# Column groups for two small projections, a closer order of the new states, and another order of the first expert loads

## The chip, the cores and the metric

The kernel runs on one core of a Trainium2 chip. The metric is the device time of one execution in microseconds (us). Before the change it is 1283.96 us, the median of three runs (1283.41 to 1284.04).

## What is computed

One layer of a hybrid decoder for 288 tokens: 256 of a prompt (two tiles of 128 rows, tile 0 and tile 1) and 32 of eight samples (tile 2). All of it is fp32. The parts that matter here:

```python
z, xbc, dt_raw, q, k, v = split_in(rmsnorm(h) @ w_in)        # dt_raw: 16 of 4112 columns
dt = softplus(dt_raw + dt_bias)                               # one step size per token and head
y_ssd, new_ssm = ssd_chunked(x, dt, -exp(a_log), B, C, old_state)
...
h = h + concat(y_ssd, attention) @ w_out
logits = rmsnorm(h) @ router_w + router_b                     # 32 columns, one per expert
top_val, top_idx = top_k(logits, 4)
...
h = h + sum over the chosen experts of gate * (swiglu(x @ w1[e] + b1[e]) @ w2[e] + b2[e])
```

There are 32 experts; w1 of one is 1024x2048 and w2 is 1024x1024, together 12.6 MB, so the experts' weights are 403 MB of the 476 MB that the kernel moves.

## The kernel before

Each engine has one program, and they meet at counting semaphores; the order on each engine is written out by hand. Time runs through four stages.

1. *Projections and attention* (to about 232 us). The list STEPS (made by mixer_steps) is walked by TensorE, VectorE and ScalarE alike. A step "proj" is eight matmuls of 288 columns, "kscore" sixteen matmuls of 288 columns whose outputs lie in four groups of 32 partitions (L1735), "pv" four matmuls of 512 columns, again in four groups of 32 (L1767), "pv_new" and "gather_o" end a group of samples, "p_score", "p_trans" and "p_out" are the prompt's attention by head. The step "dt" (L1786) takes, for each of the three tiles, eight matmuls: the stationary operand is a 128x128 block of the normed tokens xnT (128x32 for tile 2), the moving one is 16 columns of w_dt. VectorE then turns the sums into dt and dA by a chain of small operations (L1210 to L1229) with two looks at ScalarE (L887, L889), and GpSimd starts on x*dt when dt_ready is there (L652 to L655). PSUM bank 2 is shared with the steps "nat" and "conv_out".
2. *Scan and states* (to about 270 us).
3. *Output projection, new states and router* (to 351 us). mixed(c, half, order, between) is twelve matmuls of 512 columns (L1988) for one tile and one half of the columns; the dictionary between names what TensorE does ahead of its i-th matmul. In tile 0's calls these are new_states(0) to new_states(7), which make the samples' eight new states by rounds (TensorE L1911, VectorE L1317, where a round must be taken out of banks 4 and 5 before the next is written), mix_turn (transposes of the mixed rows, L1966, taken out by mixT_evac), and last_state. In tile 1's calls they are the router: router(c, ks), eight matmuls with a 128x128 block of tokens stationary and 32 columns of w_router moving (L2004), and prefix(c, s). VectorE's choose(c, s) waits for the logits, picks the four experts and signals mask_ready; prefix sums the masks; first_places gives each token its place and signals S_ready; gather_tile (L2022) then gathers the tokens of the first two experts. The last tile to be routed is tile 1.
4. *Experts* (from 351 us). Eight turns of four experts. SyncE loads units of 2 MB (six per expert, four of w1 and two of w2) into eight places; unit 8 and each one after it waits until TensorE has used the unit that lies in its place (expert_slot_used). Units 5, 6 and 7 wait for the last matmuls of mixed(1, 1). Units 0 to 3 need the places of the states, of z and of the attention's buffers: the order is 3, store_states(0), store_states(1), 0, 2, 1, 4, 5, ... by the loop below. Units 0 and 1 go where the samples' states lay, four samples each, so these have to be stored first.

```python
for n in [3, 0, 2, 1] + list(range(4, PER_EXPERT * TURN)):
    if n == 0:
        store_states(0)
        sp.wait_ge(sem("ssm_s_out"), 16 * 4)
        store_states(1)
    ...
    unit_load(e, e, j)
```

Of the kernel before, what the change touches and what calls it, by code (L numbers as in the profile page):

```python
# [11 lines left out]
ALU = mybir.AluOpType  # L12
# [124 lines left out]
def mixer_steps():  # L137
# [58 lines left out]
    steps.extend(("pv", t) for t in range(4, 8))  # L196
    steps.extend([("pv_new", 0), ("p_trans", 0), ("p_score", 1)])
# [52 lines left out]
def hymba_step(nc, a, o):  # L250

    ctx = ExitStack()
    with ctx:
# [65 lines left out]
        w_dt = d3(take(KT * H), H)  # L319
        w_router = d3(take(KT * NE), NE)  # L320
        vecs = take(36)
# [50 lines left out]
        edx = r_small[:, 144:160]  # L372
        row_max = d3(r_small[:, 0:16], DB)
# [146 lines left out]
        def _(sp):  # L520
# [222 lines left out]
        def _(act):  # L743
# [98 lines left out]
            for kind, i in STEPS:  # L842
# [41 lines left out]
                elif kind == "dt":  # L884

                    act.wait_ge(sem("dt_dve"), 1)
                    nc.scalar.activation(dts[:, 144:192], dts[:, 96:144], ACT.Exp, scale=-1.0).then_inc(sem("dt_act"), 1)  # L887
                    act.wait_ge(sem("dt_dve"), 2)
# [148 lines left out]
        def _(dve):  # L1037
# [73 lines left out]
            for kind, i in STEPS:  # L1111
# [92 lines left out]
                elif kind == "dt":  # L1204

# [3 lines left out]
                    dve.wait_ge(sem("dt_ps"), 1)  # L1209
                    nc.vector.tensor_copy(d3(vecs[:, 28:36], W1_ROWS), ps[:, 2, 48:56].rearrange("p (o s) -> p s o", o=W1_ROWS))  # L1210
                    link(nc.vector.tensor_tensor(d3(raw[:, 0:32], H), d3(ps[:, 2, 0:32], H), bvec[:, 0:16].unsqueeze(1).broadcast_to([P, 2, H]), ALU.add))
                    link(nc.vector.tensor_tensor(raw[0:NS, 32:48], ps[0:NS, 2, 32:48], bvec[0:NS, 0:16], ALU.add))
                    link(nc.vector.tensor_scalar(u1, raw, -1.0, None, ALU.mult))
                    nc.vector.tensor_tensor(u1, u1, raw, ALU.max).then_inc(sem("dt_dve"), 1)
                    dve.wait_ge(sem("dt_act"), 1)
                    nc.vector.tensor_scalar(u1, e1, 1.0, None, ALU.add).then_inc(sem("dt_dve"), 1)
                    dve.wait_ge(sem("dt_dve"), 2)
# [5 lines left out]
                    dve.wait_ge(sem("dt_act"), 2)  # L1223
# [207 lines left out]
            def choose(c, s):  # L1431

                n = ROWS[c]
                dve.wait_ge(sem("rstd_ready"), s + 2)
                dve.wait_ge(sem("logit_ps"), s + 1)
                link(nc.vector.scalar_tensor_tensor(logit[0:n, c, :], ps[0:n, LOGIT_BANK[c], 0:NE], stat[0:n, 20 + c:21 + c], bvec[0:n, 48:80], ALU.mult, ALU.add))
# [57 lines left out]
            row_scale(0, 0)  # L1494
# [3 lines left out]
            row_scale(2, 1)  # L1498
# [10 lines left out]
            row_scale(1, 2)  # L1509
# [100 lines left out]
        def _(pe):  # L1610
# [59 lines left out]
            def turn_waits():  # L1670
# [5 lines left out]
                elif turn[0] == "dt":  # L1676
                    pe.wait_ge(sem("dt_dve"), 1)

            for kind, i in STEPS:
# [99 lines left out]
                elif kind == "dt":  # L1779
# [3 lines left out]
                    nc.tensor.transpose(ps[:, 2, 48:56], rows_small[32:40, 0:P], ident[32:40, 32:40])  # L1783
# [266 lines left out]
            mixed(0, 1, natural, {1: lambda: new_states(3), 2: before_1, 4: lambda: new_states(4), 5: lambda: mix_turn(1, 1), 6: lambda: new_states(5),  # L2050
# [218 lines left out]
```

## Time and profile before

| | us |
|---|---|
| median of three runs | 1283.96 |
| the profiled execution's own time | 1286.54 |
| its span, first to last instruction | 1284.5 |
| TensorE busy (share of the span) | 1239.8 (97%) |
| VectorE, ScalarE, GpSimd busy | 383.6, 232.1, 49.2 |
| DMA moved, mean rate | 476.2 MB, 371 GB/s |

The profiled execution is 2.6 us longer than the median of the runs, and 2.0 us of it lie outside the span. A busy share is a mean over stages with different limits. "PEclk" is TensorE's granted clock, 1.00 being 2.4 GHz and 0.50 being 1.2 GHz. A matmul in fp32 stands in the rows as two instructions, so x16 are eight matmuls; transposes are one each. Rows of the timeline overlap at their ends, as matmuls are pipelined: what a group costs is best read from its start to the start of the next.

### The profile page before, as it was taken

What the parts mean: (1) busy time and instruction counts of PE and PEld (TensorE: products, weight loads), DVE (VectorE), ACT (ScalarE), POOL (GpSimd) and SP (SyncE); (2) the same over time, 40 slices, a digit from 0 to 9 for tenths busy, and PEclk for the clock granted to TensorE, in tenths of its full rate; (3) what the DMA queues carried; (4) which work ended last, traced back from release to release, by engine and by line L of the source; (5) the groups of instructions that cost most, each with busy time, mean ns of one, the idle gap of its engine ahead of it and who ended that gap; (6) DMA issues with size and microseconds to landing.
All of it is one profiled execution on the core that took longest, in us unless ns stands there. A gap on an engine that the chain in (4) does not pass through costs nothing.

```text
span 1284.5 us, 14702 instructions
## 1 busy us (share of the span) xinstructions
PE 1239.8 (97%) x5752; PEld 524.4 (41%) x5752; DVE 383.6 (30%) x768; ACT 232.1 (18%) x473; POOL 49.2 (4%) x46
## 2 busy tenths in 40 slices
PE   9999999999999999999999999999999999999997
PEld 6766665544433333333333333333333333333332
DVE  2478522674421222212132121212122221212122
ACT  2013333544201111110111011010111110110102
POOL 0000030513000000000000000000000000000000
PEclk8999989999999999999999999999999999999999
DMA  9697768336899999999999999999999999999992
GB/s 278 210 323 265 248 232 316 149 123 255 371 381 427 430 427 430 426 430 427 431 427 431 426 432 426 432 426 431 427 429 428 429 429 428 429 428 428 428 428 114
DMA packets 67294, 476.20 MB, mean 371 GB/s; under 512 B 7688, under 2 KB 25380, under 8 KB 40412
## 3 DMA queue, kind: packets, MB, share of 16 engines
q1 hardware_dynamic: 65134, 471.87, 89.5%
q10 hardware_dynamic: 1582, 2.03, 0.5%
q0 software_dynamic: 544, 1.84, 0.4%
q8 instruction: 23, 0.38, 0.1%
q14 instruction: 11, 0.09, 0.0%
HBM read 468.47 MB, written 7.24 MB: 370 GB/s over the span
## 4 chain that ended last, share of the span: by engine, by line
PE 72%; DMA 24%; DVE 2%; ACT 1%; issue 1%; SPq 0%; DVEq 0%
DMA ring<-in_w 23%; PE ps L2180 22%; PE ps L2222 13%; PE ps L1692 9%; PE ps L2128 7%; PE ps L1988 3%; PE ps L1735 1%; PE ps L2136 1%; PE ps L2112 1%; PE ps L2120 1%; PE ps L2198 1%; PE ps L2171 1%; PE ps L1767 1%; PE ps L1911 1%; PE ps L1711 1%
## 5 line engine op out<-in xcount | busy, mean ns | idle before, releaser
L2180 PE MATMUL ps<-ring,own 128*64 128x512 f32 x1536 | 340.9, 593 | 17.2 <-DMA ring<-in_w 17.2
L1581 DVE TENSOR_SCALAR own<-ps 128x512 f32<-128x512 f32 x32 | 22.2, 692 | 650.0 <-PE ps L2180 650.0
L2180 PEld LDWEIGHTS ps<-ring,own 128*64 128x64 f32 x1536 | 108.6, 137 | 236.6 <-issue 197.2
L2222 PE MATMUL ps<-ring,own 128*64 128x512 f32 x768 | 172.7, 599 | 3.5 <-ACT own L1018 3.4
L1692 PE MATMUL ps<-own,ring 128*128 128x288 f32 x512 | 132.5, 413 | 1.3 <-DVE own L1074 1.1
L2180 PE MATMUL ps<-own 128*64 128x512 f32 x512 | 115.8, 593 | 2.4 <-DMA own<-in_w 2.4
L1692 PEld LDWEIGHTS ps<-own,ring 128*128 128x128 f32 x512 | 96.2, 192 | 32.2 <-issue 4.5
L1014 ACT ACTIVATE own<-own 128x512 f32<-128x512 f32 x32 | 20.2, 631 | 444.7 <-DVE own L1581 444.7
L2222 PEld LDWEIGHTS ps<-ring,own 128*64 128x64 f32 x768 | 54.5, 138 | 107.7 <-issue 104.4
L2128 PE MATMUL ps<-own 128*128 128x512 f32 x180 | 90.0, 625 | 0.0
L1024 ACT ACTIVATE own<-ps 64x512 f32<-64x512 f32 x64 | 37.9, 593 | 230.1 <-PE ps L2222 229.3
L2180 PEld LDWEIGHTS ps<-own 128*64 128x64 f32 x512 | 36.4, 136 | 70.8 <-issue 61.2
L2222 PE MATMUL ps<-own 128*64 128x512 f32 x256 | 58.5, 598 | 2.4 <-ACT own L1018 2.4
L2128 PEld LDWEIGHTS ps<-own 128*128 128x128 f32 x180 | 29.0, 186 | 60.7 <-issue 60.7
L1988 PE MATMUL ps<-ring,own 128*128 128x512 f32 x96 | 46.6, 610 | 0.0
L1018 ACT ACTIVATE own<-ps 128x512 f32<-128x512 f32 x32 | 19.2, 599 | 106.5 <-PE ps L2198 106.5
L1152 DVE STREAM_TRANSPOSE ring<-ring 128x1024 f32<-128x1024 f32 x32 | 37.0, 1212 | 0.0
L2120 PE MATMUL ps<-own 128*128 128x512 f32 x64 | 31.8, 618 | 0.0
L2112 PE MATMUL ps<-own 128*128 128x512 f32 x64 | 31.8, 618 | 0.0
L2222 PEld LDWEIGHTS ps<-own 128*64 128x64 f32 x256 | 16.8, 135 | 32.2 <-issue 28.9
L1558 DVE COPY own<-ps 128x512 f32<-128x512 f32 x17 | 11.8, 693 | 48.3 <-PE ps L2128 47.7
L1988 PEld LDWEIGHTS ps<-ring,own 128*128 128x128 f32 x96 | 16.5, 190 | 19.5 <-issue 19.3
(353 smaller groups left out, 1009.0 us busy)
## 6 DMA issues: line engine op xcount, KB each, us to landing
ring<-in_w SPq DMA_DIRECT2D x144, 2048.0 KB, 30.6
own<-in_w SPq DMA_DIRECT2D x48, 2048.0 KB, 29.2
ring<-in_w_in SPq DMA_DIRECT2D x16, 1024.0 KB, 5.9
ring<-in_cache_win_k SPq DMA_DIRECT2D x16, 1024.0 KB, 6.6
ring<-in_cache_win_v SPq DMA_DIRECT2D x16, 1024.0 KB, 7.9
ring<-in_w_out SPq DMA_DIRECT2D x6, 1024.0 KB, 10.6
ring<-in_state_ssm SPq DMA_DIRECT2D x8, 512.0 KB, 10.5
out_ssm_sample<-ring SPq DMA_DIRECT2D x8, 512.0 KB, 4.5
```

The lines of the kernel that those rows point to most:

```text
L1014: nc.scalar.activation(sg, xg, ACT.Sigmoid, scale=ALPHA).then_inc(sem("sig_ready"), 1)
L1018: nc.scalar.activation(gT, ps[:, 0, :], ACT.Copy).then_inc(sem("gT_ready"), 1)
L1024: nc.scalar.activation(ysb[C * u:C * u + C, 512 * half:512 * half + 512], ps[C * half:C * half + C, 4, :], ACT.Copy).then_inc(sem("ysb_rea ...
L1152: last = nc.vector.transpose(to[:, k:k + 2], rows[:, k:k + 2])
L1581: nc.vector.tensor_scalar(xg_o, hid[:, 0], LIMIT, None, ALU.min).then_inc(sem("glu_ready"), 1)
L1692: last = nc.tensor.matmul(ps[:, i % 2, 0:TOK], w[:, k, (i % 2) * P:(i % 2) * P + P], xnT[:, k, :], start=(k == 0), stop=(k == KT - 1))
L1988: last = nc.tensor.matmul(ps[:, h_bank(c, half), :], mixT[:, k, cols(c)], w_rows(k)[:, 512 * half:512 * half + 512], start=(i == 0), stop= ...
L2112: nc.tensor.matmul(ps[:, 6 + half, :], GT[:, cols(0)], ysb[:, 512 * half:512 * half + 512], start=True, stop=True)
L2120: last = nc.tensor.matmul(ps[:, 1 + half, :], GT[:, cols(1)], ysb[:, 512 * half:512 * half + 512], start=True, stop=True)
L2128: last = nc.tensor.matmul(ps[:, 6 + half, :], S1[0:n, c, :], xn[0:n, c, 512 * half:512 * half + 512], start=(c == 0), stop=(c == 2))
L2180: last = nc.tensor.matmul(ps[C * half:C * half + C, 1 + m, :], xT[:, k, C * u:C * u + C], rows[:, D * half + 512 * m:D * half + 512 * m + ...
L2222: last = nc.tensor.matmul(ps[C * half:C * half + C, 4, :], gT[:, (k % 4) * P + C * (k // 4):(k % 4) * P + C * (k // 4) + C], rows[:, 512 * ...
```

## The change

Three parts.

*dt and the router turned round.* The weights are now stationary and the tokens move. Block k of the weights goes to column group k mod 4, so that its sums land in partitions 32g to 32g+31 of the bank; each group sums two of the eight blocks. The four partial sums are copied to SBUF (dt_parts by ScalarE, logit_parts by VectorE) and a second small matmul with group_sum, a 128x32 matrix with four ones in each column, adds them and turns them back to tokens by columns. For dt the second step is a new kind "dt_sum", four pv steps after "dt"; for the router it is router_sum, placed one or two matmuls after router. dt's stationary blocks are 32 wide, of which 16 columns count.

*New states closer together.* In mixed(0, 1) the rounds 3 to 7 stand ahead of matmuls 1, 3, 5, 7 and 9 (before: 1, 4, 6, 8 and 11), and the mix_turns and last_state ahead of 0, 2, 6 and 4 (before: 2, 5, 9 and 7). VectorE takes tile 1's mix turns out one round earlier.

*Loads.* SyncE asks for units 0, 4 and 2 ahead of store_states(1), and unit 4 ahead of 2 and 1.

```diff
     steps.extend(("pv", t) for t in range(4, 8))
+    steps.append(("dt_sum", 0))
     steps.extend([("pv_new", 0), ("p_trans", 0), ("p_score", 1)])
...
+        dt_cols = [own[:, w_dt_at + H * k:w_dt_at + H * k + 32] for k in range(KT)]
...
+        group_sum = rows_small[:, P:P + NE]
+        logit_parts = rows_small[:, 0:P]
+        dt_parts = sub(r_o, 0, TOK)
...
-            for n in [3, 0, 2, 1] + list(range(4, PER_EXPERT * TURN)):
+            for n in [3, 0, 4, 2, 1] + list(range(5, PER_EXPERT * TURN)):
                 e, j = n // PER_EXPERT, n % PER_EXPERT
                 if n == 0:
                     store_states(0)
                     sp.wait_ge(sem("ssm_s_out"), 16 * 4)
-                    store_states(1)
                 elif n == 2:
                     sp.wait_ge(sem("y_sums"), 9)
                     sp.wait_ge(sem("fin_out"), 16)
                 elif n == 1:
+                    store_states(1)
                     sp.wait_ge(sem("ssm_s_out"), 16 * 8)
...
                 elif kind == "dt":
-
-                    act.wait_ge(sem("dt_dve"), 1)
+                    act.wait_ge(sem("dt_ps"), 1)
+                    act.wait_ge(sem("score_ps"), DB)
+                    nc.scalar.activation(dt_parts, ps[:, 2, 0:TOK], ACT.Copy).then_inc(sem("dt_act"), 1)
+                elif kind == "dt_sum":
+
+                    act.wait_ge(sem("dt_dve"), 2)
                     nc.scalar.activation(dts[:, 144:192], dts[:, 96:144], ACT.Exp, scale=-1.0).then_inc(sem("dt_act"), 1)
...
                 elif kind == "dt":
+                    dve.wait_ge(sem("head_ps"), 4)
+                    nc.vector.tensor_reduce(group_sum, ident.rearrange("p (g c) -> p c g", g=4), AX_X, ALU.add).then_inc(sem("dt_dve"), 1)
+                elif kind == "dt_sum":
...
             def choose(c, s):
 
                 n = ROWS[c]
+                dve.wait_ge(sem("logit_ps"), 2 * s + 1)
+                nc.vector.tensor_copy(logit_parts[:, 0:n], ps[:, LOGIT_BANK[c], 0:n]).then_inc(sem("logit_rows"), 1)
+                row_scale(c, s)
                 dve.wait_ge(sem("rstd_ready"), s + 2)
-                dve.wait_ge(sem("logit_ps"), s + 1)
...
             new_states(2)
             add_mixed(0, 0)
+            mixT_evac(1, 0)
             new_states(3)
-            mixT_evac(1, 0)
             new_states(4)
             new_states(5)
+            mixT_evac(1, 2)
             new_states(6)
-            mixT_evac(1, 2)
             new_states(7)
...
+                    for k in range(KT):
+                        g = k % 4
+                        last = nc.tensor.matmul(ps[32 * g:32 * g + 32, 2, 0:TOK], dt_cols[k], xnT[:, k, :], start=(k < 4), stop=(k >= 4))
+                    last.then_inc(sem("dt_ps"), 1)
+                elif kind == "dt_sum":
+                    pe.wait_ge(sem("dt_act"), 1)
+                    pe.wait_ge(sem("dt_dve"), 1)
                     for c in range(3):
-                        for k in range(KT):
-                            last = nc.tensor.matmul(ps[0:ROWS[c], 2, H * c:H * c + H], xnT[:, k, cols(c)], w_dt[:, k, :], start=(k == 0), stop=(k == KT - 1))
+                        last = nc.tensor.matmul(ps[0:ROWS[c], 2, 320 + H * c:320 + H * c + H], dt_parts[:, cols(c)], group_sum[:, 0:H], start=True, stop=True)
                     last.then_inc(sem("dt_ps"), 1)
...
                 for k in ks:
-                    last = nc.tensor.matmul(ps[0:n, LOGIT_BANK[c], 0:NE], xnT[:, k, cols(c)], w_router[:, k, :], start=(k == 0), stop=(k == KT - 1))
+                    g = k % 4
+                    last = nc.tensor.matmul(ps[NE * g:NE * g + NE, LOGIT_BANK[c], 0:n], w_router[:, k, :], xnT[:, k, cols(c)], start=(k < 4), stop=(k >= 4))
                 if KT - 1 in ks:
                     last.then_inc(sem("logit_ps"), 1)
+
+            def router_sum(c, s):
+                n = ROWS[c]
+                pe.wait_ge(sem("logit_rows"), s + 1)
+                nc.tensor.matmul(ps[0:n, LOGIT_BANK[c], 256:256 + NE], logit_parts[:, 0:n], group_sum, start=True, stop=True).then_inc(sem("logit_ps"), 1)
...
-            mixed(0, 1, natural, {1: lambda: new_states(3), 2: before_1, 4: lambda: new_states(4), 5: lambda: mix_turn(1, 1), 6: lambda: new_states(5),
-                                  7: last_state, 8: lambda: new_states(6), 9: lambda: mix_turn(1, 2), 11: lambda: new_states(7)})
+            mixed(0, 1, natural, {0: before_1, 1: lambda: new_states(3), 2: lambda: mix_turn(1, 1), 3: lambda: new_states(4), 4: last_state,
+                                  5: lambda: new_states(5), 6: lambda: mix_turn(1, 2), 7: lambda: new_states(6), 9: lambda: new_states(7)})
...
-            mixed(1, 0, natural, {1: first_router, 5: sample_turn, 9: sample_router, 11: lambda: prefix(0, 0)})
+            mixed(1, 0, natural, {1: first_router, 3: lambda: router_sum(0, 0), 5: sample_turn, 7: sample_router, 9: lambda: router_sum(2, 1), 11: lambda: prefix(0, 0)})
...
             router(1, range(4, KT))
-            gather_tile(0, 0)
+            gather_tile(0, 0, (0,))
+            router_sum(1, 2)
+            gather_tile(0, 0, (1,))
             prefix(1, 2)
```

## Rows read from the trace of the kernel before

**Rows 1.** The page, part 2: GB/s that the DMA engines moved, 40 slices of 32 us.
```profile
GB/s 278 210 323 265 248 232 316 149 123 255 371 381 427 430 427 430 426 430 427 431 427 431 426 432 426 432 426 431 427 429 428 429 429 428 429 428 428 428 428 114
```

**Rows 2.** The chain that ended last, its end: start us, us, what.
```profile
1203.71 7.02 PE ps L2222 x32
...
1218.24 33.13 DMA ring<-in_w
...
1259.65 8.77 PE ps L2222 x32
```

**Rows 3.** A window: stretch, length, PE busy (instructions), PEclk, DMA share, GB/s.
```profile
350.00:355.00 5.00, 4.38 (x24) 1.00 0.00 0
```

**Rows 4.** Line L578, SyncE's unit loads 7 and 8: issue time, and time to landing.
```profile
L578 SPq DMA_DIRECT2D ring<-in_w x1: 328/328/328, 337.8 to 337.8; - x1
...
DMA to landing us min/median/max: 13.0/13.0/13.0
...
L578 SPq DMA_DIRECT2D ring<-in_w x1: 328/328/328, 354.7 to 354.7; - x1
...
DMA to landing us min/median/max: 7.8/7.8/7.8
```

**Rows 5.** Windows of TensorE over tile 0's output projection and new states.
```profile
270.00:305.00 35.00, 34.96 (x123) 1.00 0.55 188
```

**Rows 6.** Timeline of TensorE around dt and at a later pv: start, us, form.
```profile
167.92 5.30 PE L1786 MATMUL ps<-own 128*128 128x16 f32 x47
...
173.22 5.79 PE L1767 MATMUL ps<-ring 128*32 128x512 f32 x29
...
211.41 3.64 PE L1767 MATMUL ps<-ring 128*32 128x512 f32 x32
```

**Rows 7.** Windows of TensorE around dt and the last router, columns as in the windows above.
```profile
165.00:170.00 5.00, 5.00 (x35) 1.00 0.58 158
...
172.00:177.00 5.00, 5.00 (x46) 0.50 0.17 33
...
341.00:345.00 4.00, 4.00 (x11) 0.57 0.97 409
```

**Rows 8.** The chain at its beginning: start us, us, what.
```profile
61.47 2.08 PE ps L1735 x32
63.55 4.09 PE ps L1692 x16
67.97 3.90 PE ps L1692 x16
```

**Rows 9.** Timeline of VectorE: the first and the last operation of dt's chain.
```profile
173.38 0.17 DVE L1210 COPY own<-ps 128x8 f32<-128x8 f32 x1 [5.71 <-PE ps L1786]
...
177.71 0.21 DVE L1229 TENSOR_TENSOR own<-own 128x48 f32<-128x48 f32 x1
```

**Rows 10.** One round of new states on VectorE (timeline).
```profile
288.22 1.66 DVE L1317 SCALAR_TENSOR_TENSOR ring<-ring,own,ps 128x256 f32<-128x256 f32 x4 [0.70 <-PE ps L1911]
```

**Rows 11.** Timeline of SyncE: unit 0 is asked for.
```profile
308.90 1.29 SPq L578 DMA_DIRECT2D ring<-in_w  x1
```

**Rows 12.** Timeline of TensorE: the router of tiles 0 and 2 and the last of tile 1.
```profile
312.30 1.87 PE L2004 MATMUL ps<-own 128*128 128x32 f32 x16
314.00 3.68 PE L1988 MATMUL ps<-ring,own 128*128 128x512 f32 x8
...
321.86 0.69 PE L2004 MATMUL ps<-own 128*32 128x32 f32 x16
...
340.34 1.08 PE L2004 MATMUL ps<-own 128*128 128x32 f32 x8
341.26 3.56 PE L2022 MATMUL ps<-own 128*128 128x512 f32 x4
```

**Rows 13.** Timeline of VectorE: tile 1's mask is made, and its places start.
```profile
342.94 0.37 DVE L1444 TENSOR_REDUCE own<-own 128x32 f32<-128x128 f32 x1
...
345.83 0.19 DVE L1452 SCALAR_TENSOR_TENSOR own<-ps,own 128x32 f32<-128x32 f32 x1 [2.52 <-PE ps L2015]
```

More of the change, by code:

```diff
@@ L318, in hymba_step @@
         cw = d3(sub(r_Bcw, 3 * G * N, CT * 29), 29)
-        w_dt = d3(take(KT * H), H)
+        w_dt_at = used[0]
+        r_dt = take(KT * H)
+        w_dt = d3(r_dt, H)
         w_router = d3(take(KT * NE), NE)
+        dt_cols = [own[:, w_dt_at + H * k:w_dt_at + H * k + 32] for k in range(KT)]
         vecs = take(36)
@@ L884, in _ @@
                 elif kind == "dt":
-                    act.wait_ge(sem("dt_dve"), 1)
+                    act.wait_ge(sem("dt_ps"), 1)
[3 more added lines that the diff above has]
+                    act.wait_ge(sem("dt_dve"), 2)
                     nc.scalar.activation(dts[:, 144:192], dts[:, 96:144], ACT.Exp, scale=-1.0).then_inc(sem("dt_act"), 1)
-                    act.wait_ge(sem("dt_dve"), 2)
+                    act.wait_ge(sem("dt_dve"), 3)
                     nc.scalar.activation(dts[:, 192:240], dts[:, 96:144], ACT.Ln).then_inc(sem("dt_act"), 1)
@@ L1208, in _ @@
                     dve.wait_ge(zeroed, 2)
[L1209 to L1212, printed above, removed]
+                    dve.wait_ge(sem("dt_ps"), 2)
+                    nc.vector.tensor_copy(d3(vecs[:, 28:36], W1_ROWS), ps[:, 2, 368:376].rearrange("p (o s) -> p s o", o=W1_ROWS))
+                    link(nc.vector.tensor_tensor(d3(raw[:, 0:32], H), d3(ps[:, 2, 320:352], H), bvec[:, 0:16].unsqueeze(1).broadcast_to([P, 2, H]), ALU.add))
+                    link(nc.vector.tensor_tensor(raw[0:NS, 32:48], ps[0:NS, 2, 352:368], bvec[0:NS, 0:16], ALU.add))
                     link(nc.vector.tensor_scalar(u1, raw, -1.0, None, ALU.mult))
                     nc.vector.tensor_tensor(u1, u1, raw, ALU.max).then_inc(sem("dt_dve"), 1)
-                    dve.wait_ge(sem("dt_act"), 1)
+                    dve.wait_ge(sem("dt_act"), 2)
                     nc.vector.tensor_scalar(u1, e1, 1.0, None, ALU.add).then_inc(sem("dt_dve"), 1)
-                    dve.wait_ge(sem("dt_dve"), 2)
+                    dve.wait_ge(sem("dt_dve"), 3)
                     link(nc.vector.tensor_scalar(dt, u1, -1.0, None, ALU.add))
@@ L1222, in _ @@
                     link(nc.vector.tensor_tensor(dA, dA, e1, ALU.mult))
-                    dve.wait_ge(sem("dt_act"), 2)
+                    dve.wait_ge(sem("dt_act"), 3)
                     link(nc.vector.reciprocal(u1, dt))
@@ L1433, in choose @@
                 n = ROWS[c]
+                dve.wait_ge(sem("logit_ps"), 2 * s + 1)
+                nc.vector.tensor_copy(logit_parts[:, 0:n], ps[:, LOGIT_BANK[c], 0:n]).then_inc(sem("logit_rows"), 1)
+                row_scale(c, s)
                 dve.wait_ge(sem("rstd_ready"), s + 2)
-                dve.wait_ge(sem("logit_ps"), s + 1)
-                link(nc.vector.scalar_tensor_tensor(logit[0:n, c, :], ps[0:n, LOGIT_BANK[c], 0:NE], stat[0:n, 20 + c:21 + c], bvec[0:n, 48:80], ALU.mult, ALU.add))
+                dve.wait_ge(sem("logit_ps"), 2 * s + 2)
+                link(nc.vector.scalar_tensor_tensor(logit[0:n, c, :], ps[0:n, LOGIT_BANK[c], 256:256 + NE], stat[0:n, 20 + c:21 + c], bvec[0:n, 48:80], ALU.mult, ALU.add))
                 link(nc.vector.max(top8[0:n, c, :], logit[0:n, c, :]))
@@ L1676, in turn_waits @@
                 elif turn[0] == "dt":
-                    pe.wait_ge(sem("dt_dve"), 1)
+                    pe.wait_ge(sem("dt_dve"), 2)
             for kind, i in STEPS:
@@ L1782, in _ @@
                     turn[:] = [kind, i]
-                    nc.tensor.transpose(ps[:, 2, 48:56], rows_small[32:40, 0:P], ident[32:40, 32:40])
+                    nc.tensor.transpose(ps[:, 2, 368:376], rows_small[32:40, 0:P], ident[32:40, 32:40])
+                    for k in range(KT):
[5 more added lines that the diff above has]
+                    pe.wait_ge(sem("dt_dve"), 1)
                     for c in range(3):
-                        for k in range(KT):
-                            last = nc.tensor.matmul(ps[0:ROWS[c], 2, H * c:H * c + H], xnT[:, k, cols(c)], w_dt[:, k, :], start=(k == 0), stop=(k == KT - 1))
+                        last = nc.tensor.matmul(ps[0:ROWS[c], 2, 320 + H * c:320 + H * c + H], dt_parts[:, cols(c)], group_sum[:, 0:H], start=True, stop=True)
                     last.then_inc(sem("dt_ps"), 1)
```

3 lines of the change are left out of this document (removed).

## The prediction, made before the changed kernel was built or run

> **What bounds the kernel now.** I began with the page's slices [rows 1]: from the thirteenth slice on, at 385 us, the DMA engines move 426 to 432 GB/s in every slice but the last, so the experts' stage is a stream of weights at one rate. The chain that ended last agrees [rows 2]: its last long piece is 33 us of waiting for weights, after which TensorE only finishes. TensorE's busy share of 97% is no proof that it sets the end.
>
> The next question is what sets the start of that stream. There the windows [rows 3] show a hole: between 350 and 355 us nothing moves. The loads explain it [rows 4]. Unit 7, the last that has a free place, was asked for at 337.8 and landed 13.0 later, at 350.8. Unit 8 needs a place that TensorE frees with its first used unit, and was asked for at 354.7. From there on the stream never stops: 184 units of 2.1 MB at 428 GB/s are 901 us, which leads to 1256, beside the last waits for weights. So the end is the moment of the first freed place plus a constant, and the first freed place is 3.5 us of matmuls behind the start of the first expert at 351.2. All that TensorE saves ahead of 351 us comes off the end one for one, as long as the eight first units have landed by then. What a load asked for earlier saves by itself is nothing: it would only widen the hole.
>
> So the sum is a sum over TensorE's path from 168 to 351 us. In that stretch it is almost never idle: [rows 5] has 34.96 of 35 us, and where it waits, it waits for engines that it itself feeds.
>
> **dt.** Before: 24 matmuls in 5.30 us [rows 6], 0.22 each, for 16 columns. Then come sixteen pv matmuls in 5.79 us, where the same sixteen take 3.64 us at 211 us. The difference is the clock [rows 7]: 1.00 before dt, 0.50 (1.2 GHz) from 172 to 177 us, though TensorE was busy all of the time and had no idle stretch. What came before the fall was only matmuls of 16 columns.
> After: eight matmuls of 288 columns in four column groups. The nearest rows are kscore's [rows 8], the same shape: sixteen in 2.08 us, so eight in 1.04. dt_sum adds three matmuls of 16 columns, 3 x 0.22 = 0.66. A projection right behind a kscore took 4.09, others 3.90: 0.19 is what a change from column groups to the whole array costs, and dt_sum brings one more. Four tiny matmuls of "sums", 0.2, hide in the 5.30 and stay. Saved: 5.30 - 1.04 - 0.66 - 0.19 - 0.2 = 3.2 us. If the clock stays up, pv gives 5.79 - 3.64 = 2.15 more. I take it in full, 5.35 in all: the some 5 us of 16-column matmuls are what stood ahead of the fall, and of them 1.7 us (1.04 of it dense) is left. Bounds: 3.2 if the clock still falls. Above, kscore's time would have to shrink, which no row suggests.
> The Trainium skill (TensorEngine Tiling (Array Packing), Key Properties) speaks against it: changing the tiling mode drains the TensorE. By that rule dt_sum and each router group pay for their switches; the trace agrees, and prices one at 0.19 us, as in the sum.
> The Trainium skill (TensorE: Matmul & The Clock Gate, Why this matters for your kernels) ties a fall of the clock to idle gaps between bursts of matmuls. By that, dt with no gap would not be the cause, the fall would stay, and dt would save 3.2 us; the rows, a fall in a stretch that is busy throughout, go against it.
>
> What else hangs on dt. VectorE's chain is 4.5 us long [rows 9]. It now starts after dt_sum, at 167.9 + 1.0 + 0.2 + 3.6 + 0.85 = 173.6, so dt_ready comes at 178.1 as before, while everything on TensorE is 5.35 us earlier. Queued behind the chain on VectorE are pv_new's scaling (0.75) and p_score(1) (1.1), done near 180.0, with ScalarE's exponentials at 181.1. TensorE needs the first for gather_o(0) behind proj(28), at 180.2, and the second for p_trans(1) at 182.0. Both fit, with about 1 us to spare: nothing. GpSimd's x*dt takes 11.5 us from dt_ready and is asked for only after 200 us. The ScalarE copy (about 0.4) and VectorE's reduction lie under the 3.6 us of pv. The DMA loads of w_in and v in this stage follow TensorE's own releases and move with it.
>
> **New states.** One round holds VectorE for 1.66 us [rows 10] and TensorE for 1.06; between two rounds there will be two matmuls of 0.88 and a transposing turn of 0.45 or so, 2.2 us against 1.66 plus two hand-overs of 0.15. So no new stall, or one of 0.2 at round 7, where VectorE first has a mix turn to take out. And no gain: TensorE does the same instructions, without idle time before [rows 5]. Zero; bounds -0.2 and +0.5. What is earlier is the end of round 7, by 3 us, and with it the second store.
>
> **Loads.** Unit 0 was asked for at 308.9 [rows 11], behind both stores. It moves to about 291 (290.7 when the first stores land), 4 and 2 follow, the second stores queue behind 6 MB, some 15 us, and land near 312; then unit 1, and 5, 6, 7 when mixed(1, 1) frees them, as before. Unit 7 lands near 336 instead of 350.8, for a first expert at 344. Worth nothing now, as the first freed place still rules. Without this part the hole would shrink from 3.9 us to about 2, and still be there. If SyncE hangs at fin_out or the second stores, it has some 20 us of cover before unit 1 is late.
>
> **Router.** Tile 0: 1.70 us from 312.30 to 314.00 [rows 12] for eight matmuls with 128-wide stationary blocks. Tile 2 has 32-wide blocks and takes 0.62 to 0.69. Weights now are 32 wide, and 128 moving columns in four groups need 8 x 0.13 x 128/288 = 0.46, so loading the weights rules: 0.62. Added: a switch, 0.19, and router_sum, 0.24. Saved 0.65. Tile 2: 0.62 stays, sum and switch are added: -0.4. Tile 1, first half: 0.81 becomes 0.31 + 0.19, saved 0.3. Together 0.55; bounds 0.1 and 1.0. VectorE's copies: add_mixed_sample ends at 314.3 in old times, the copy at 314.6, router_sum is due at 314.6. Tile 2 moved from matmul 9 to 7, with the transposed tokens ready 1.2 us ahead. No stall over 0.2.
>
> **The tail.** Here latencies rule, not TensorE. Before: router's second half at 340.34, tile 1's mask ready at 343.31, its places start at 345.83 [rows 13], 5.5 us later, because gather_tile(0, 0) took 3.56 us [rows 12] at a clock of 0.57 [rows 7] in place of 1.8, and prefix stood behind it. After, at full clock: router 0.3, VectorE's copy done at 0.8, one gather half until 1.1, router_sum 1.35, mask at 3.3, prefix and places at 3.75. Saved 1.7. At half clock: gather half until 2.0, sum 2.4, mask 4.35, places 5.0: saved 0.45. The stretch ahead of the old fall, gathers with 32 rows, transposes and the router, mostly stays, and TensorE will now wait a microsecond for the mask; so half of it: 1.1.
>
> **Sum.** 5.35 + 0 + 0 + 0.55 + 1.1 = 7.0 us. The profiled execution of 1286.54 would be 1279.5; the same saving off the median of 1283.96 gives 1276.9 us.
>
> **The rivals.**
> 1. *The clock still falls in or behind dt*, and at the tail: 3.2 + 0.55 + 0.45 = 4.2, so 1279.8 us. For it: small matmuls and transposes remain on both sides of dt. Against: those sides ran at 1.00 before. It is also the result of the skill's rule on gaps. Chance 0.17.
> 2. *No fall at all, at the end neither.* The last w2 took 8.77 us where others take 7.02 [rows 2]. If the fall there misses it, 1.75 goes too, with a tail at full clock: 9.35, so 1274.6. Chance 0.15.
> 3. *A new wait eats the gain*: VectorE's dt chain, 4.5 us, is 1 us from being exposed, and column groups might overlap less here than in kscore (3.9 instead of 1.04 us for dt). The first would cost 3.5 us, the second 2.9: 1280.2 by their mean. Chance 0.08.
> 4. *The end does not follow TensorE*, because the stream is fed by something fixed. Same time, 1284. Against: the hole. Chance 0.03.
> 5. *Slower: the small matmuls pull the clock down where it was full.* Each of router's three sums adds 32-column work and a wait in the dense output projection. Dt's fall lasted 6.8 us and cost half of that. Three such falls in the dense matmuls cost 10.2, against the 5.9 us that are left when the tail's 1.1 is gone: 1288.3. At 1.7 falls it would be level. Against: tile 0's router, 1.7 us of 32-column matmuls, let the clock stand at 1.00. Chance 0.02.
>
> The forecast has 0.55. The range reaches from rival 2 with the routers at their better bound, 1274.0, to rival 1 with half a microsecond of stalls, 1280.3; about 0.14 is outside. About 0.2% (2.6 us) is what a measurement of this kernel tells from no change: a saving of 3 is faster. Faster 0.94, same 0.04, slower 0.02.
>
> **What would show it.** Right: L1786 with 16 instructions in about 1 us and the pv behind it in 3.6; PEclk at 1.00 from 165 to 180; GpSimd's first operation still at 178; no new idle on TensorE at gather_o or p_trans; the first expert at about 344; a DMA hole of 8 to 10 us before it; the last wait for weights 7 us earlier. Wrong: a wait of TensorE for VectorE around 180 or 315, units landing after the first expert starts, or a fall of the clock in the middle of the output projection.

## The result, and the profile after

The changed kernel took 1275.55 us, median of four runs (1273.57 to 1276.34), against 1283.68 for the kernel before in the same comparison: a ratio of 0.9939, 95% interval 0.9917 to 0.9961. In a later comparison with more runs the same two kernels gave 1279.64 (eleven runs, 1275.5 to 1281.3) and 1283.83 (22 runs): 0.9962, 0.9943 to 0.9981. The change is faster in both; the forecast, 7.0 us off the time before, lies between the two savings of 8.1 and 4.2 us. Why the two differ is one of the findings below.

| us | before | after |
|---|---|---|
| profiled execution's own time | 1286.54 | 1276.34 |
| its span | 1284.5 | 1274.5 |
| first projection starts | 15.74 | 14.22 |
| dt starts | 167.76 | 166.16 |
| dt to the first p_trans | 12.17 | 6.46 |
| first router to the last router | 28.04 | 26.83 |
| last router to tile 1's places | 5.49 | 4.07 |
| dt to the first expert, in all | 182.86 | 174.44 |
| first expert to the last used unit of w1 | 900.79 | 899.89 |
| from there to the end | 33.09 | 34.01 |

The page (part 1 and two lines of part 2: PEclk, and GB/s in slices of 32 us) shows the same stream of weights as [rows 1], 427 to 429 GB/s. The hole now lies in the eleventh slice: 304 GB/s there and 423 in the twelfth, against 371 and 381 before, so the start of the stream is fed no better than before.

```profile
span 1274.5 us, 14670 instructions
PE 1228.5 (96%) x5732; PEld 515.4 (40%) x5732; DVE 384.6 (30%) x772; ACT 232.3 (18%) x474; POOL 49.2 (4%) x46
PEclk9999999999999999999999999999999999999998
GB/s 279 234 323 262 244 261 345 89 160 348 304 423 429 427 427 428 428 428 428 428 429 428 428 428 429 429 428 429 429 428 428 428 429 429 428 428 428 427 428 110
```

TensorE's timeline of the stretch of [rows 6] (start, us, form; the new lines are L1800 for dt, L1806 for dt_sum, L1781 for pv) and VectorE's chain, as in [rows 9]:

```profile
166.31 1.18 PE L1800 MATMUL ps<-own 128*32 128x288 f32 x16
167.31 0.22 PE L1768 MATMUL ps<-own 128*32 128x1 f32 x8
167.37 3.62 PE L1781 MATMUL ps<-ring 128*32 128x512 f32 x32
170.92 0.78 PE L1806 MATMUL ps<-own 128*128 128x16 f32 x6
171.63 1.06 PE L1788 MATMUL ps<-own,ring 32*32 32x512 f32 x8
172.62 0.55 PE L1833 MATMUL ps<-own,ring 128*128 128x128 f32 x3
...
171.81 0.17 DVE L1224 COPY own<-ps 128x8 f32<-128x8 f32 x1 [3.99 <-PE ps L1806]
...
176.13 0.21 DVE L1243 TENSOR_TENSOR own<-own 128x48 f32<-128x48 f32 x1
```

From start to start dt is 1.06 us with the tiny sums, pv 3.55, dt_sum 0.71, and nothing waits. The windows (stretch, length, PE busy and instructions, PEld, DVE, ACT, POOL, PEclk, DMA share, GB/s) have the clock at 1.00 where [rows 7] have 0.50, and the hole of [rows 3] again:

```profile
165.00:170.00 5.00, 5.00 (x62) 2.34 (x64) 0.90 (x3) 1.32 (x7) 0.00 (x0) 1.00 0.63 181
172.00:177.00 5.00, 5.00 (x29) 3.29 (x22) 3.77 (x17) 3.43 (x5) 0.57 (x1) 1.00 1.06 392
340.00:345.00 5.00, 4.40 (x24) 1.70 (x26) 1.20 (x4) 1.28 (x1) 0.00 (x0) 1.00 0.00 0
```

The routers, as in [rows 12] (L2025 router, L2032 router_sum, L2008 the output projection):

```profile
304.86 0.65 PE L2025 MATMUL ps<-own 128*32 128x128 f32 x16
305.43 1.98 PE L2008 MATMUL ps<-ring,own 128*128 128x512 f32 x4
307.25 0.30 PE L2032 MATMUL ps<-own 128*128 128x32 f32 x2
...
311.81 0.33 PE L2025 MATMUL ps<-own 128*32 128x32 f32 x16
312.07 1.98 PE L2008 MATMUL ps<-ring,own 128*128 128x512 f32 x4
...
331.69 0.43 PE L2025 MATMUL ps<-own 128*32 128x128 f32 x8
332.05 1.13 PE L2048 MATMUL ps<-own 128*128 128x512 f32 x2
333.01 0.30 PE L2032 MATMUL ps<-own 128*128 128x32 f32 x2
333.15 1.10 PE L2048 MATMUL ps<-own 128*128 128x512 f32 x2
334.09 0.64 PE L2039 MATMUL ps<-own 128*128 128x32 f32 x4
335.25 0.41 PE L2041 MATMUL ps<-own 128*128 128x32 f32 x2 [0.52 <-DVE own L1461]
```

VectorE at the tail, as in [rows 13], and SyncE's queue, as in [rows 11]: L585 are the expert loads, L575 the stores of states.

```profile
334.83 0.37 DVE L1461 TENSOR_REDUCE own<-own 128x32 f32<-128x128 f32 x1
335.76 0.19 DVE L1469 SCALAR_TENSOR_TENSOR own<-ps,own 128x32 f32<-128x32 f32 x1 [0.56 <-PE ps L2041]
...
289.97 0.36 SPq L585 DMA_DIRECT2D ring<-in_w  x1
290.38 1.97 SPq L585 DMA_DIRECT2D own<-in_w  x2
296.45 1.99 SPq L575 DMA_DIRECT2D out_ssm_sample<-ring  x4
314.53 30.49 SPq L585 DMA_DIRECT2D ring<-in_w  x5
```

Unit 0 is asked for at 290.0, not 308.9, and unit 7 lands at 339.9 (329.1 and 10.8 us). Unit 8 is asked for at 344.7: 4.8 us of hole, where it was 3.9. The end of the chain, beside [rows 2], still is one wait for weights and then TensorE:

```profile
1207.33 33.12 DMA ring<-in_w
1240.49 3.68 PE ps L2208 x16
...
1249.05 9.37 PE ps L2250 x32
```

### The profile page after: what moved, and what is told of

The parts are those of the page before. It is cut to its first block, busy times and chain, and to the rows that moved or that the text cites. A ratio compares the mean times of both kernels' runs of the same rounds, so it can differ in the third digit from the quotient of the medians.

```text
span 1274.5 us, 14670 instructions
## 1 busy us (share of the span) xinstructions
PE 1228.5 (96%) x5732; PEld 515.4 (40%) x5732; DVE 384.6 (30%) x772; ACT 232.3 (18%) x474; POOL 49.2 (4%) x46
## 4 chain that ended last, share of the span: by engine, by line
PE 71%; DMA 25%; DVE 2%; ACT 1%; issue 1%; SPq 0%; DVEq 0%
DMA ring<-in_w 23%; PE ps L2208 23%; PE ps L2250 13%; PE ps L1706 9%; PE ps L2156 7%; PE ps L2008 3%; PE ps L1749 1%; PE ps L2164 1%; PE ps L2148 1%; PE ps L2140 1%; PE ps L2226 1%; DMA ring<-in_w_in 1%; PE ps L2199 1%; PE ps L1931 1%; PE ps L1725 1%
## 5 line engine op out<-in xcount | busy, mean ns | idle before, releaser
L2156 PEld LDWEIGHTS ps<-own 128*128 128x128 f32 x180 | 29.0, 186 | 60.7 <-issue 60.7
L2008 PE MATMUL ps<-ring,own 128*128 128x512 f32 x96 | 47.1, 612 | 0.0
L2226 PEld LDWEIGHTS ps<-own 128*128 128x128 f32 x128 | 15.0, 143 | 23.7 <-issue 23.7
```

The lines of the kernel that those rows point to most:

```text
L2008: last = nc.tensor.matmul(ps[:, h_bank(c, half), :], mixT[:, k, cols(c)], w_rows(k)[:, 512 * half:512 * half + 512], start=(i == 0), stop= ...
L2156: last = nc.tensor.matmul(ps[:, 6 + half, :], S1[0:n, c, :], xn[0:n, c, 512 * half:512 * half + 512], start=(c == 0), stop=(c == 2))
L2226: last = nc.tensor.transpose(ps[:, 0, j * P:(j + 1) * P], gg[:, j * P:(j + 1) * P], ident)
```

## The experiments

Milestones in the text are read from TensorE's timeline of each kernel. "Granted clock" is the mean over an execution.

### dt alone

Everything but dt's turning round is as before the change.

```diff
-            mixed(0, 1, natural, {0: before_1, 1: lambda: new_states(3), ...
+            mixed(0, 1, natural, {1: lambda: new_states(3), 2: before_1, ...
-                    last = nc.tensor.matmul(ps[NE * g:NE * g + NE, LOGIT_BANK[c], 0:n], w_router[:, k, :], xnT[:, k, cols(c)], ...)
+                    last = nc.tensor.matmul(ps[0:n, LOGIT_BANK[c], 0:NE], xnT[:, k, cols(c)], w_router[:, k, :], ...)
-            for n in [3, 0, 4, 2, 1] + ...
+            for n in [3, 0, 2, 1] + ...
```

> The kernel before with dt's part of the change alone. Theory: from the start of dt to the transposes behind pv_new it takes 6.3 us in place of 12.0, no fall of the clock between, and nothing of it is lost on the way: the first expert starts 5.7 us earlier counted from the start of dt, and the time is 5.7 us shorter, 1278. Rival (the change as a whole is needed, since the weight loads would set the end without their new order): less than 4 us. Rival (the 10 us of the profile are mostly the clock's luck at the start): under 3 us.

Measured: 1274.55 us (ten runs; 1278 was expected) against 1283.56, ratio 0.9945 (0.9926 to 0.9963). Dt to p_trans is 6.46 us, 5.7 less than before. The tail's fall was absent too, without any change there: last router to places took 3.79 us. So dt carries most of the gain, and the tail's clock isn't the router's doing. In this comparison the two kernels below have 1277.38 and 1276.55 us, so in the medians nothing is seen of what the router and the new order add to dt.

### The router as before

```diff
-                nc.tensor.matmul(ps[0:n, LOGIT_BANK[c], 256:256 + NE], logit_parts[:, 0:n], group_sum, start=True, stop=True).then_inc(sem("logit_ps"), 1)
...
-            gather_tile(0, 0, (0,))
-            router_sum(1, 2)
-            gather_tile(0, 0, (1,))
+            gather_tile(0, 0)
```

> The changed kernel with the router of before: tokens stationary, no router_sum. Theory: 1.2 us come back in the output projection and 1.4 in the tail, so 2.6 us slower than the changed kernel, 1278.2; of the tail's part most is the clock, so PEclk should be under 1.00 somewhere between the second half of tile 1's router and the first expert. Rival (the tail's fall was a matter of where the clock's check fell, not of the router): the clock stays at 1.00 and only about 1.5 us come back, 1277.

Measured: 1277.38 us, ratio 0.9955 (0.9933 to 0.9978), and the clock stayed at 1.00 in the tail, as the rival had it. In the trace dt to the first expert is 175.36, 0.92 us more than with the router turned round: 1.2 more from the first to the last router, 0.27 less from there to the places. TensorE's tail, with the clock at 1.00:

```profile
334.38 1.08 PE L2024 MATMUL ps<-own 128*128 128x32 f32 x8
335.30 1.97 PE L2042 MATMUL ps<-own 128*128 128x512 f32 x4
```

gather_tile takes 1.97 us where it took 3.56 [rows 12], with the old router ahead of it. The new tail is no shorter than this one: it is 0.3 us longer.

### New states and loads as before

```diff
-            for n in [3, 0, 4, 2, 1] + list(range(5, PER_EXPERT * TURN)):
+            for n in [3, 0, 2, 1] + list(range(4, PER_EXPERT * TURN)):
-            mixed(0, 1, natural, {0: before_1, 1: lambda: new_states(3), 2: lambda: mix_turn(1, 1), ...
+            mixed(0, 1, natural, {1: lambda: new_states(3), 2: before_1, 4: lambda: new_states(4), ...
```

> The changed kernel with the new states and the loads in the order of before (dt and router as changed). Theory: both are worth nothing: TensorE does the same work, and unit 7 lands near 343, still ahead of the first freed place at 344.7; the time is the changed kernel's, 1275.5, within 0.5. The hole in the DMA stream shrinks from some 9 us to 2 or 3. Rival (the loads set the start of the stream): 2 to 3 us slower.

Measured: 1276.55 us, ratio 0.9942 (0.9923 to 0.9962), and 174.58 us from dt to the first expert against 174.44. By these two traces the new order is worth nothing. What the order does do is seen at the units: with the old order unit 7 lands at 342.0 and unit 8 is asked for at 342.5, so the hole is all but gone (2 to 3 us were expected), and yet no unit is late.

```profile
340.00:345.00 5.00, 5.00 (x26) 1.75 (x24) 0.00 (x0) 0.00 (x0) 0.00 (x0) 1.00 0.37 85
```

### The loads' order with less TensorE work ahead

Two kernels to find where the order starts to count: ten of tile 1's 24 matmuls with w_out are left out in both; the second also has new states and loads as before.

```diff
+                    if c == 1 and i in (2, 4, 6, 8, 10):
+                        continue
```

> The changed kernel with ten of tile 1's 24 matmuls with w_out left out (so tile 1's mixed rows and all that follows are not the reference's), to bring the first expert 8.6 us earlier. Theory: the end follows TensorE as long as the eight first units are in; they are (unit 7 asked for 6 us earlier than in the changed kernel), so the time is 8 us shorter, 1267.5. Rival (the stream is fed by something fixed): 1275.5.

> The same ten matmuls left out, but new states and loads in the order of before. Theory: now unit 7 lands at about 343 and the first place is freed at 336, so the stream has no hole left and rules from unit 0 on: 4 to 5 us slower than with the new order, 1272. So the order of loads is worth nothing today and up to 5 us once TensorE is earlier. Rival (the loads are hidden at any rate): as with the new order, 1267.5.

Measured: 1270.32 us (ratio 0.9893, 0.9861 to 0.9924) and 1271.26 us (0.9917, 0.9886 to 0.9949). In the first (1267.5 was expected), dt to the first expert is 6.7 us shorter than in the changed kernel (167.73): the router's stretch lost 7.8, and a fall of the clock behind it, 0.65 from 328 to 332 us, gave some back. From dt to the end of the span it is 5.9 us shorter (the span lost another 0.8 ahead of dt, which isn't this change's): the end follows TensorE. With the old order unit 7 landed at 343.6, behind unit 8's asking, and unit 8 took 10.3 us to land in place of 7.7. Both, as line L585 shows them, new order first:

```profile
L585 SPq DMA_DIRECT2D ring<-in_w x1: 328/328/328, 337.6 to 337.6; - x1
DMA to landing us min/median/max: 7.7/7.7/7.7
...
L585 SPq DMA_DIRECT2D ring<-in_w x1: 327/327/327, 338.2 to 338.2; - x1
DMA to landing us min/median/max: 10.3/10.3/10.3
```

The loads' order is worth 2.6 us there by this row, 1.6 us in the sum of the two stretches up to the last w1 unit, and the medians (0.9 apart, intervals overlapping) don't resolve it. I had expected 4 to 5 us. The new order is insurance: with the old one and TensorE's full work 0.5 us were left between unit 7 and unit 8, and it pays from there on.

### dt in one column group

```diff
-                        last = nc.tensor.matmul(ps[32 * g:32 * g + 32, 2, 0:TOK], dt_cols[k], xnT[:, k, :], start=(k < 4), stop=(k >= 4))
+                        last = nc.tensor.matmul(ps[0:32, 2, 0:TOK], dt_cols[k], xnT[:, k, :], start=(k == 0), stop=(k == KT - 1))
...
```

(ScalarE's copy and dt_sum read 32 partitions in place of 128.)

> The changed kernel with all eight of dt's matmuls in the same column group, so that they cannot run beside each other. Same 288 columns, same 32-wide weights. Theory: concurrency of the four groups is what makes them cheap: eight take 8 x 0.487 = 3.9 us in place of 1.06, the clock stays at 1.00, and the time is 2.9 us more, 1278.4. Rival (turning the operands round is enough, and the groups add nothing): 1275.5.

Measured: 1280.45 us (1278.4 was expected), ratio 0.9967 (0.9947 to 0.9987). Dt to p_trans is 9.24 us, 2.78 more than in four groups, near the 2.9 expected: the same eight matmuls (nearly all in this row) don't overlap.

```profile
168.37 3.84 PE L1799 MATMUL ps<-own 128*32 128x288 f32 x15
...
167.00:177.00 10.00, 10.00 (x80) 4.51 (x78) 1.15 (x5) 1.30 (x7) 0.00 (x0) 1.00 0.62 184
```

The clock stays at 1.00 with them, so it isn't the column groups that hold it up, but wide matmuls in place of 16-column ones. Its tail, with the new router, has a fall (0.70 from 340 to 345 us).

### dt as before, but in two pieces

All 24 matmuls of 16 columns, eight ahead of the first four pv steps and sixteen behind them; the rest of the kernel as before.

```diff
...
+                    dt_tiles([0])
+                elif kind == "dt_rest":
+                    dt_tiles([1, 2])
```

> The kernel before, with dt's 24 matmuls as they are, but tile 0's eight ahead of the four pv steps and the other sixteen behind them. No instruction less. Theory: it is the unbroken 5 us of 16-column matmuls that brings the clock down; apart, the clock stays at 1.00, dt costs 1.7 + 2.4 and pv 3.6 us, 7.7 in place of 11.1, and the time is 3 us shorter, 1281. Rival (the fall comes with something else of that stretch): the same clock, the same time, 1283.7.

Measured: 1282.90 us against 1283.64, ratio 0.9998 (0.9982 to 1.0013); 1281 was expected. The fall didn't vanish. It came later, 2.0 us behind the last of the 24, and was half as long (TensorE's two pieces, then windows):

```profile
167.83 1.96 PE L1684 MATMUL ps<-own 128*128 128x16 f32 x16
...
173.36 2.57 PE L1684 MATMUL ps<-own 128*128 128x16 f32 x32
...
168.00:173.00 5.00, 5.00 (x56) 2.69 (x56) 0.17 (x1) 0.36 (x3) 0.00 (x0) 1.00 0.87 251
...
176.00:181.00 5.00, 5.00 (x22) 2.81 (x16) 3.74 (x17) 3.43 (x5) 0.35 (x1) 0.69 1.05 390
```

Dt's stage was 3.0 us shorter, the stretch behind it 1.6 longer. My expectation of 1.00 throughout was wrong: spreading the small matmuls shortened the fall and did not prevent it. The trace has a second use. Both pieces ran at 1.00, so they price the 24 matmuls at full clock: 1.89 and 2.49 us to the start of what follows, 4.4 in all. The kernel before took 5.3 for them [rows 6], because its fall began inside dt. Its window 168 to 173 us has 2.2 us at half clock, which puts the fall at 170.8, 2.9 us behind dt's first matmul:

```profile
168.00:173.00 5.00, 5.00 (x46) 4.96 (x47) 0.00 (x0) 0.45 (x4) 0.00 (x0) 0.78 0.77 213
```

### 24 small matmuls put back

The changed kernel, and ahead of dt's eight wide matmuls another 24 of 16 columns whose results nobody reads.

```diff
+                    for k in list(range(KT)) * 3:
+                        nc.tensor.matmul(ps[:, 2, 400:416], xnT[:, k, 0:P], w_dt[:, k, :], start=True, stop=True)
```

> The changed kernel with 24 matmuls of 128x16 columns, whose results nobody reads, put back ahead of the time steps' eight. Both theories: about +5.1 us at 0.11 us a matmul plus its load. Theory (TensorE's clock fell at 170.6 us before because of the unbroken run of small matmuls, though the engine was busy): a stretch at half clock comes in or just behind the time steps, and another 1.7 to 3.4 us, 1282 to 1284 in all. Rival (the fall had another cause): clock 1.00 throughout, 1280.6.

Measured: 1285.70 us (1282 to 1284 was expected) against 1279.64 for the changed kernel on the same chip, +6.1 us. The stage from dt to p_trans is 13.53 us, 7.07 more:

```profile
164.18 5.77 PE L1799 MATMUL ps<-own 128*128 128x16 f32 x48
169.88 2.15 PE L1802 MATMUL ps<-own 128*32 128x288 f32 x16
...
168.00:173.00 5.00, 5.00 (x48) 3.06 (x51) 0.17 (x1) 0.41 (x1) 0.00 (x0) 0.66 0.07 22
```

The 24, all with 128-wide stationary blocks, take 5.70 us to the start of the eight wide ones, all but the last 0.6 of it at full clock. The other 1.4 is a stretch of 3.4 us at 1.2 GHz that is back (0.66 in the window, so 3.4 of 5 us at 0.50), with TensorE busy for 5.00 of 5.00 us: the eight wide matmuls, that took 1.0 us, now take 1.9. This is the plainest evidence for the cause of dt's fall, though that one lasted twice as long.

The other traces bear it out. In each of the eleven with dt turned round PEclk is 1.00 from 160 to 185 us; the three that have 24 matmuls of 16 columns there all have a fall, at 170.8, 177.9 and 169.3 us. What in these matmuls does it, the few moving columns or the loading of as many stationary blocks (PEld is busy 4.96 of 5.00 us in the window above), no run separates.

### Falls at the end and at the start

First the end. In the last turn TensorE waits 1.2 us for the last unit and 2.9 us for VectorE, and part of the last w2 runs at half clock. Three wide matmuls that nobody reads fill the second wait.

```diff
+                    if ending and r == TURN - 1:
+                        for _ in range(3):
+                            stay_busy(7, 512)
```

> The changed kernel plus three matmuls of 512 columns into an unused bank in the last expert, while TensorE waits 2.9 us for VectorE's product. Their results are not used. Theory: the last w2 takes 9.37 us instead of 7.0 and the transposes ahead of it 1.1 instead of 0.6 because the clock fell in this wait; filled, the clock stays up and 2 to 2.8 us go, 1273. Rival (the fall has been set off by the thin work before, or lies within the run's noise): no change, or 0.3 us slower if the fill delays the transposes.

Measured: 1275.22 us (ratio 0.994, 0.9918 to 0.9962; 1273 was expected), not to be told from the changed kernel's 1275.55, though in the trace the last w2 took 7.09 us in place of 9.37 and the stretch from the last w1 to the end 31.39 in place of 34.01. The two medians are from different comparisons; so the changed kernel was run again, together with this one and one with a busier start (more warm-up ahead, and two wide matmuls before the first projection):

```diff
-            for i in range(6):
+            for i in range(9):
...
+            pe.wait_ge(sem("xnT_act"), 4)
+            for _ in range(2):
+                stay_busy(3, 256)
```

> The changed kernel as it is, on one chip with the three below, for a paired comparison. Both theories: a median near 1275.5 us and a ratio near 0.994 to the kernel before. If time follows the granted clock, its single executions lie on one line, time = 1270.5 us + 1280 us x (1 - mean granted clock), within about 1 us; if it does not, they scatter about it by more.

> The changed kernel with the end's thin waits filled with matmuls nobody reads (as in e8). Theory: the 6.8 us at half clock near the end of the stream is gone in every execution, so the median is 2 to 3 us below the changed kernel's on this chip and the mean clock higher by about 0.002. Rival (the end is set by the transfers of the last unit, and TensorE's clock there is not what matters): within 0.7 us of it.

> e10 plus a busier start: nine warm-up matmuls instead of six, and two matmuls of 256 columns that nobody reads ahead of the first projection. Theory: the fall near 20 to 26 us of the trace (10.2 us at half clock in the kernel before, 3.4 in the changed one) goes, the first projection starts at 13.9 to 14.2 us, and the median falls by another 2 to 4 us, to about 1269 to 1272. Rival: the fall belongs to the transposes behind the first projection, or the added matmuls delay the start by what they save: within 0.7 us of e10.

Measured, on one chip: the changed kernel 1279.64 (ratio 0.9962, 0.9943 to 0.9981; some 1275.5 was expected), with the busy end 1274.36 (0.992, 0.9899 to 0.9942), with both 1274.14 (0.9923, 0.9902 to 0.9944). The windows at the end, changed kernel, then busy end:

```profile
1235.00:1262.00 27.00, 21.31 (x81) 6.67 (x78) 4.82 (x9) 3.45 (x6) 0.00 (x0) 0.87 0.56 237
...
1235.00:1262.00 27.00, 24.09 (x98) 8.13 (x95) 4.82 (x9) 4.18 (x6) 0.00 (x0) 1.00 0.64 271
```

The busy end gains 5.3 us in the medians here and 2.9 in the two traces (31.40 against 34.33 from the last w1 on). The 2.9 are the fill's: the three traces with it have 1.00 in this window, and the eleven without it all have a fall there. The rest is not: the mean granted clocks of the two sets of runs, 0.9965 and 0.992, lie 0.0045 apart, and some 7 us at half clock make 0.0027. Over both comparisons the 12 runs with the busy end have a mean of 1274.5 and the changed kernel's 15 have 1278.0. The start, changed kernel, then both ends:

```profile
10.00:24.00 14.00, 12.93 (x43) 8.80 (x43) 4.97 (x15) 3.40 (x8) 0.00 (x0) 0.63 1.08 348
...
10.00:24.00 14.00, 13.95 (x72) 10.13 (x72) 5.70 (x17) 3.82 (x10) 0.00 (x0) 1.00 1.08 346
```

The clock at the start is 1.00 in this trace, but that alone doesn't show that the fill did it: four of the thirteen traces whose start is not filled have 1.00 there too, among them the first trace with the busy end alone. The runs say more. None of the six with both ends has a mean granted clock under 0.997, which is at most some 8 us at half clock in the whole execution (9 by the rounding), so none can have had the long fall of 10 us; with the busy end alone they go down to 0.994. And yet the median is the same: the rival's number holds. The traces with 1.00 at the start show a price: the first projection starts at 14.72 us with the fill and at 13.94 to 14.43 without. So filling the end is worth some 3 us; for the start no gain is shown. In this comparison both versions beat the changed kernel by more than 5 us in the medians; in the first one the busy end's ratio, 0.994, was no better than the changed kernel's 0.9939.

## Why the prediction was right, by its own steps

**The bound.** Right. The hole is there, [rows 3] and 340 to 345 us after, and where TensorE's path to the first expert was cut by 6.7 us the end came 5.9 earlier, counted from dt. Rival 4, an end that doesn't follow TensorE, falls with it.

**dt.** 5.35 us forecast, 5.7 measured: the total was right, its split was not. kscore's rate held (1.0 us for eight), and dt_sum with its switches cost 0.71 instead of 0.85. The term that was mis-sized is the old one. I took the 24 matmuls' 5.30 us as their cost at full clock and put the fall behind them, but it began inside, at 170.8, and at full clock they cost 4.4. From dt's first matmul to pv_new it was 11.0 us before, 8.0 with dt in two pieces at full clock and 5.3 after: 2.7 us are instructions (3.2 forecast) and 3.0 are clock (2.15 forecast). The two errors largely cancel. The reason that I gave for an absent fall was weaker than it read, too: not some 5 us of 16-column matmuls stood ahead of the fall, but 2.9, against the 1.7 that are left. The steps themselves were tested: dt alone has the same dt to p_trans, 6.46 us, one column group shows that the overlap of the groups is worth 2.8 of it, and the 24 small matmuls put back bring a fall back. Rivals 1 and 5 did not occur: PEclk is 1.00 from 165 to 180 us and through the output projection. Nor did rival 3: p_score(1) was done on VectorE at 177.9 and p_trans(1) on TensorE was due near 180.

**The skill's rule on the clock.** The Trainium skill (TensorE: Matmul & The Clock Gate, Why this matters for your kernels) ties falls to idle gaps between bursts. The traces speak against that as the only cause: at dt, before the change and with the small matmuls put back, TensorE was busy for 5.00 of the 5.00 us of the window in which the clock fell. At the end of the kernel they agree with it: there gaps of 1.2 and 2.9 us stand around it, and filling the second removed it.

**New states and loads.** Zero forecast, zero measured (174.58 against 174.44). The hole widened, but from 3.9 to 4.8 us only, where I had named 8 to 10 as a sign: I put unit 7's landing at 336, it was 339.9, and unit 8 was asked for at 344.7. With the old order the hole was 0.5 us, not 2.

**Router.** 0.55 us forecast, 1.2 measured, outside my upper bound of 1.0. The term that was mis-sized is the loading of the weights: I took tile 2's 0.62 us as its floor. With four column groups the same sixteen instructions took 0.57 for tile 0 and 0.26 for tile 2, so loads overlap across groups too. Tiles 0 and 2 and tile 1's first half gave 1.13, 0.36 and 0.45; router_sum took back 0.14 and 0.18, and the rest, 0.4, went to the dense matmuls next to them, 0.1 at each change between the groups and the whole array.

**The tail.** 1.1 forecast, 1.4 measured, and for the wrong reason. Its instructions got 0.3 us longer, not shorter: at full clock the old tail takes 3.79. What the trace gained is the clock, 1.7 us, and that fall is absent with the old router as well. My step "half of it", which tied it to the small work in the tail, was wrong; such a fall comes and goes between executions of the same tail. Of the four traces with the old one only the kernel before has it, of the ten with the new one four have it (one column group, both kernels with less TensorE work, and one of the two with only the end filled, where the places to the first expert take 6.53 us against 4.88 in the other). In these four it comes behind the places, and the last router to the places still takes 4.07. So that the tail's gain came near the forecast is luck. Of rival 2 the end's part did not come: the last w2 took 9.37 us.

**The sum.** From dt to the first expert the trace gained 8.4 us: 5.7 + 1.2 + 1.4 and 0.1 elsewhere; 3.7 of it are instructions (2.7 at dt, 1.2 and 0.1, less 0.3 in the tail) and 4.7 clock. The span gained 10.0, since dt started 1.6 earlier (1.5 of it at the first projection) and the stream was 0.9 shorter, and the end 0.9 longer. None of those three need belong to the change: in the thirteen traces with an unfilled start the first projection begins between 13.9 and 16.2 us, in all fourteen the stream takes 899.5 to 901.4, and the unfilled ends take 32.8 to 34.3.

**What I did not foresee: how much of the time is the granted clock.** The 31 executions of the kernel before that ran beside dt alone go from 1277.23 us at a granted clock of 0.997 to 1289.08 at 0.987, and scatter about a line by 0.6 us (root mean square; 1.5 at most): some 12 us for 0.010. Part of that is arithmetic, as a stretch at half clock lengthens what TensorE does and lowers the mean clock together. The line that I had put on record for the changed kernel's second set missed: nine of its eleven executions lie 1.7 to 2.8 us below it. In the second comparison the changed kernel had 0.992 in the mean of its eleven executions, the kernel before 0.9919 of its 22: the same, although dt's fall was gone, and its trace has 10 us at half clock at the start, where the first trace of it has 3.4. At an equal clock of 0.992 the lines give 1283.6 and 1279.0: 4.6 us, where the traces have 3.7 of instructions. The interval of that comparison is 2.4 to 7.3 us, so the two agree and more can't be said. In the first comparison the clock was 0.996, and the saving was 8.1. So what the trace gained in clock, 4.7 us, is true of the traced execution and may be of the first comparison, but not of every one. Nor is each fall of the trace before in every execution: at 0.997 there are some 8 us at half clock in all, and the traced one, at 0.99, has some 26. That the median came out near the forecast owes something to this, and is luck to that extent. What decides between executions whether a fall comes isn't settled.

## What to carry to other kernels

A matmul that moves few columns costs its overhead: turn it round, so that the weights stand and the tokens move, put the blocks into column groups and add the groups by one more small matmul; read its price from a step of the same shape in the same trace, and look up the granted clock of the row that gives the price, old or new. Before counting a fall of the clock as gain, find out whether it is there in more than the one traced execution, and compare kernels at an equal granted clock. And when transfers wait for places, asking for them in a better order is worth nothing until the compute path is short enough.

## What was unexpected in the hardware

- TensorE's clock fell from 2.4 to 1.2 GHz while the engine was busy throughout: 2.9 us into a run of 16-column matmuls, 5.1 us into one, and 2.0 us behind the second of two short runs. Fifteen of the sixteen instructions of dt in one group, 288 columns wide and 3.84 us long, left it at 1.00.
- Sixteen fp32 instructions with 32-wide stationary blocks and 32 moving columns take 0.62 us from start to start in one column group and 0.26 in four.
- A change between column groups and the whole array cost about 0.1 us around the router, not 0.19.
- Runs that look like noise of 10 us are mostly mean granted clock, which each run lists: 0.010 of it is 9 us in the changed kernel's eleven and 10 to 12 in the sets of the kernel before.
